# Moving two modulation terms from TensorE to GpSimd in the prologue of a two-layer decoder trunk

## What is computed

```python
cond = jax.nn.silu(c)                          # 1024 values
for l in range(DEPTH):                         # 2 layers
    mod = cond @ w_mod[l] + b_mod[l]           # 1024 x 3072 product with one row
    shift, scale, gate = thirds of mod
    h = rmsnorm(x, norm_g[l]) * (1.0 + scale) + shift
    P = h @ w_in[l]                            # one wide projection, cut into heads
    ...                                        # three mixers, gated and merged
    x = x + gate * (merged @ w_out[l])
return rmsnorm(x, final_g)
```

## Time and profile before

| | |
|---|---|
| runs | 1308.01, 1309.58, 1309.88 us; median 1309.58 |
| the profiled execution's own time | 1307.09 us |
| its span in the trace | 1305.3 us |
| PE busy | 1273.2 us, 98% of the span |
| DVE, ACT, POOL busy | 692.4, 630.3, 719.2 us |
| mean granted PE clock | 0.997 of full |
| first column 0 on PE to the end of the five items | 17.5 to 64.0 us |

### The profile page before, as it was taken

How to read it: one execution, slowest core, us unless ns; L and a number is a source line. 1 busy time by engine, 2 the same in 40 slices (tenths; PEclk the granted TensorE clock), 3 DMA queues, 4 the chain that set the end, 5 groups by cost and what they waited for, 6 DMA issues and landing times.

```text
span 1305.3 us, 16860 instructions
## 1 busy us (share of the span) xinstructions
PE 1273.2 (98%) x5772; PEld 1006.7 (77%) x5772; DVE 692.4 (53%) x1129; ACT 630.3 (48%) x958; POOL 719.2 (55%) x1470
## 2 busy tenths in 40 slices
PE   7999999999999999999999999999999999999996
PEld 4878887787678777788868888778876777778885
DVE  7677767634757234444365777553356533333332
ACT  5366656444553344444245666554455424344441
POOL 3365556774335554576645645576623474546662
PEclk9999999999999999999999999999999999999999
DMA  9432223342223433342222111223311232332331
GB/s 367 148 87 81 65 67 119 113 142 95 73 73 122 133 101 110 101 129 97 97 74 97 66 65 65 90 92 105 112 56 55 83 113 81 93 93 81 97 97 65
DMA packets 40902, 130.51 MB, mean 100 GB/s; under 512 B 5392, under 2 KB 5520, under 8 KB 39536
## 3 DMA queue, kind: packets, MB, share of 16 engines
q1 hardware_dynamic: 30448, 110.22, 25.8%
q10 hardware_dynamic: 10368, 19.21, 5.0%
HBM read 126.33 MB, written 2.10 MB: 98 GB/s over the span
## 4 chain that ended last, share of the span: by engine, by line
PE 89%; DVE 5%; ACT 2%; DMA 1%; POOL 1%; issue 1%; SPq 0%; DVEq 0%; ACTq 0%
PE ps_st L831 22%; PE ps_st L833 22%; PE ps_st L832 22%; PE ps_o L897 5%; PE ps_s L935 3%; PE ps_s L978 3%; PE ps_s L1001 2%; PE ps_misc L892 1%; PE ps_w L987 1%; DMA pro_w<-w_mod_first 1%; POOL w_lo L697 1%; ACT w_hi L1066 1%; PE ps_s L937 1%; PE ps_w L1013 0%; DVE sq_sum L1426 0%
## 5 line engine op out<-in xcount | busy, mean ns | idle before, releaser
L697 POOL TENSOR_TENSOR w_lo<-raw,w_hi 128x128 fp32r<-128x128 f32 x1448 | 708.4, 526 | 563.7 <-ACT w_hi L1066 563.6
L831 PE MATMUL ps_st<-h_hi,w_hi 128*128 128x512 f32 x920 | 372.7, 405 | 3.2 <-POOL w_lo L697 2.7
L833 PE MATMUL ps_st<-h_hi,w_lo 128*128 128x512 f32 x920 | 359.1, 390 | 0.0
L832 PE MATMUL ps_st<-h_lo,w_hi 128*128 128x512 f32 x920 | 358.6, 390 | 0.0
L1066 ACT ACTIVATE w_hi<-raw 128x1024 fp32r<-128x1024 f32 x182 | 190.5, 1047 | 70.9 <-PE ps_st L833 41.2
L831 PEld LDWEIGHTS ps_st<-h_hi,w_hi 128*128 128x128 f32 x920 | 172.9, 188 | 44.9 <-POOL w_lo L697 5.5
L832 PEld LDWEIGHTS ps_st<-h_lo,w_hi 128*128 128x128 f32 x920 | 173.0, 188 | 38.4 <-issue 4.8
L833 PEld LDWEIGHTS ps_st<-h_hi,w_lo 128*128 128x128 f32 x920 | 172.7, 188 | 36.9
L1388 DVE TENSOR_SCALAR gate_x<-ps_st 128x512 f32<-128x512 f32 x79 | 54.4, 689 | 198.2 <-PE ps_st L833 197.9
L1088 ACT ACTIVATE gate_t<-gate_x 128x512 f32<-128x512 f32 x80 | 50.5, 631 | 220.8 <-DVE gate_x L1388 219.9
L1090 ACT ACTIVATE gate_t<-gate_t,cs 128x512 f32<-128x512 f32 x80 | 57.9, 724 | 2.7
(11 more groups left out here) (317 smaller groups left out, 2028.5 us busy)
## 6 DMA issues: line engine op xcount, KB each, us to landing
raw<-w_stream SPq DMA_DIRECT2D x178, 512.0 KB, 3.5
mod_w<-w_mod ACTq DMA_DIRECT2D x64, 256.0 KB, 2.7
pro_w<-w_mod_first SPq DMA_DIRECT2D x8, 1024.0 KB, 16.0
x<-x_t SPq DMA_DIRECT2D x4, 512.0 KB, 7.4
ret_decay<-decay ACTq DMA_DIRECT2D x2, 1024.0 KB, 4.8
out_t<-o_t SPq DMA_DIRECT2D x8, 256.0 KB, 2.9
raw<-w_stream SPq DMA_DIRECT2D x4, 384.0 KB, 3.0
raw_extra<-w_stream SPq DMA_DIRECT2D x2, 512.0 KB, 19.9
```

Of the source, the lines that this page charges most:

```text
L697: ins = nc.gpsimd.tensor_tensor(lo[:, r], whole[:, r], hi[:, r].bitcast(F32), ALU.subtract)
L831: nc.tensor.matmul(dst[0:m, :], wh, hi, start=(k == 0), stop=False)
L832: nc.tensor.matmul(dst[0:m, :], wh, lo, start=False, stop=False)
L833: last = nc.tensor.matmul(dst[0:m, :], wl, hi, start=False, stop=(k == nk - 1))
```

## The change

Terms 6 and 7 of every block go from PE to POOL. A new function `last_terms(j)` on POOL waits for `pro_w[j]`, multiplies both terms by cond into SBUF (`pro_p`, `pro_q`, which lie in `gate_x` and `gate_t`), waits for its own two results, adds them, and signals `pro_part`. It stands twice at the head of POOL's queue, once after each of the first five w_lo, and once more after the fifth. DVE's first term of block j waits for `pro_part`, and adds POOL's partial sum: `tensor_scalar` becomes `scalar_tensor_tensor` with a second operand from SBUF. PE's columns keep only the products with ones.

```diff
+        pro_p, pro_q = gate_x[:, :, 0:2 * P], gate_t[:, :, 0:2 * P]
...
         @block.gpsimd
         def _(pool):
+            def last_terms(j):
+                pool.wait_ge(pro_in[j % MOD_RING], 16 * (j // MOD_RING + 1))
+                if j == 0:
+                    pool.wait_ge(cond_ready, 1)
+                if j >= 2:
+                    pool.wait_ge(pro_mod_done, j - 1)
+                for k in range(DVE_TERMS, DT):
+                    src, by = pro_w[:, j % MOD_RING, k, :], cond[:, k:k + 1]
+                    dst = (pro_p if k == DVE_TERMS else pro_q)[:, j % 2, :]
+                    nc.gpsimd.tensor_scalar(dst, src, by, None, ALU.mult).then_inc(pro_part_link, 1)
+                pool.wait_ge(pro_part_link, (DT - DVE_TERMS) * (j + 1))
+                nc.gpsimd.tensor_tensor(pro_p[:, j % 2, :], pro_p[:, j % 2, :], pro_q[:, j % 2, :], ALU.add).then_inc(pro_part, 1)
+
+            last_terms(0)
+            last_terms(1)
             for layer in range(DEPTH):
...
                     ins.then_inc(w_lo_ready, 1)
+                    if layer == 0 and i < len(BATCH):
+                        last_terms(i + 2)
+                        if i == len(BATCH) - 1:
+                            last_terms(DT - 1)
...
                 def mod_columns(j):
-                    pe.wait_ge(pro_in[j % MOD_RING], 16 * (j // MOD_RING + 1))
-                    if j == 0:
-                        pe.wait_ge(cond_ready, 1)
                     columns_of = [bank["w1"][:, what * DT + j:what * DT + j + 1] for what in range(2)]
                     pe.wait_ge(pro_mod_done, j + 1)
                     for what, dst in enumerate(columns_of):
-                        for k in range(DVE_TERMS, DT):
-                            nc.tensor.matmul(dst, pro_w[:, j % MOD_RING, k, what * P:(what + 1) * P], cond[:, k:k + 1],
-                                             start=(k == DVE_TERMS), stop=False)
                         last = nc.tensor.matmul(dst, pro_acc[:, j % 2, what * P:(what + 1) * P], ones[:, 0:1],
-                                                start=False, stop=True)
+                                                start=True, stop=True)
                     last.then_inc(pro_mod_sum, 1)
...
                         if k == 0:
                             dve.wait_ge(pro_in[j % MOD_RING], 16 * (j // MOD_RING + 1))
-                            link(V.tensor_scalar(acc, src, by, None, ALU.mult))
+                            dve.wait_ge(pro_part, j + 1)
+                            link(V.scalar_tensor_tensor(acc, src, by, pro_p[:, j % 2, :], ALU.mult, ALU.add))
```

More of the change, by code:

```diff
@@ L612, in build @@
         names = ("early_in", "const_in", "pos_in", "par_in", "cond_e", "cond_ready", "pro_link", "pro_mod_done",
-                 "pro_mod_sum", "angles", "tables", "tables_in", "tables_mla", "pro_sq", "fin_sum", "fin_link",
+                 "pro_mod_sum", "angles", "tables", "tables_in", "tables_mla", "pro_sq", "pro_part", "pro_part_link", "fin_sum", "fin_link",
                  "fin_rstd", "fin_wide", "fin_x", "fin_out", "fin_pool", "stored")
         (early_in, const_in, pos_in, par_in, cond_e, cond_ready, pro_link, pro_mod_done, pro_mod_sum, angles, tables,
-         tables_in, tables_mla, pro_sq, fin_sum, fin_link, fin_rstd, fin_wide, fin_x, fin_out, fin_pool, stored) = (sem(n) for n in names)
+         tables_in, tables_mla, pro_sq, pro_part, pro_part_link, fin_sum, fin_link, fin_rstd, fin_wide, fin_x, fin_out, fin_pool, stored) = (sem(n) for n in names)
         pro_in = [sem(f"pro_in{i}") for i in range(MOD_RING)]
```

## The result

| | before | changed |
|---|---|---|
| median of the runs | 1309.69 us (1308.01 to 1309.88) | 1318.9 us (1316.76 to 1321.11) |
| ratio, 95% interval | | 1.0067 (1.005 to 1.0084) |
| the profiled execution's own time, span | 1307.09, 1305.3 | 1318.2, 1316.4 |
| column 7 over (first step behind it starts) | 54.22 us | 63.74 us |
| mean granted PE clock | 0.997 | 0.990 |

The account below looks back on a forecast made before the run. POOL's queue was to set the prologue's pace: 17.4 + 6 x 1.98 + 5 x 4.03 = 49.4 us, then block 6 on DVE and PE's steps to column 7 at 59.6 against 54.22. That is +5.4 us, 1315.0, range 1311.0 to 1319.5.

Parts of the forecast that it names:

- What bounds it, and the mechanism: Prologue: from block 2 on POOL sets the pace, period 6.01 us against DVE's 4.66; column 7 ends 5.4 us later.
- The case with 50%: The forecast itself: L from 1.52 to 2.3 us, without a fall of PE's clock that costs.
- L: Time of POOL's three new instructions per block, two products, a wait and a sum: 1.98 us; shift is 6 L - 6.5 us.
- The price of the product: POOL's 128x256 product with a scalar: 0.43 us, between bounds of 0.155 and 0.70, before the prologue's factor.
- The factor 1.18 for the prologue: POOL is slower in the prologue than at the end, 4.03 / 3.42; the three instructions go from 1.56 to 1.84 us.
- The extra operand on DVE: DVE's first term reads two tensors from SBUF and contends with POOL: up to 0.26 us for block 6, 0.1 counted.
- The columns on PE: Each PE column falls from 1.25 to 0.44 us; columns 3 to 7 save at most 4.05 us.
- Covered work: Later pro_w 6 and 7 transfers cost nothing; POOL's first w_lo ends at 23.4, before PE took it at 23.95, thin cover.
- POOL keeping up: Rival: POOL's instructions overlap or L is below 1.08, so the columns' saving decides: -2.2 us, 1307.4; 4%.
- cheap products: Rival on POOL's products: L from 1.08 to 1.52, 1310 to 1312.2 us; 14%.
- Dear products: Rival: product as dear as a sum or dearer, or contention delaying POOL; L above 2.3, +7.3 us and more; 17%.
- The clock: Rival: PE's waits before columns lower its clock, and behind column 6 that adds 1.7 us, 1316.7; 15%.

Follow-up runs that it names:

- e2: Changed kernel with POOL's new work done but neither waited for nor used by DVE, and PE's columns as before: 1313.37 us, 1.0021 against the kernel before.
- e3: Changed kernel with one 128x512 tensor_tensor on POOL, cond broadcast, in place of the two tensor_scalar products: 1314.67 us, 1.0034 against the kernel before.
- e5: Changed kernel with only term 7 on POOL, no sum, and term 6 kept on PE: ratio 0.9983 against the kernel before.
- e1: Changed kernel with terms 6 and 7 left out altogether, so no POOL part and no DVE wait for it: 1304.38 us, 0.996 against the kernel before.
- e12: The changed kernel measured again unaltered, in more rounds: 1317.24 us, 1.0057 against the kernel before.

## Why the prediction came out as it did

**What bounds it, and the mechanism: right.** The end of the stretch is set by six parts and five w_lo in POOL's queue, then block 6 on DVE, then seven steps and column 7 on PE. The profile after shows this chain step for step, e2 shows that without DVE's wait 5.2 of the 9.5 us go and only 1.9 of the rest is POOL's late w_lo, and e3 and e5 show that DVE's block 6 follows the part's length about sixfold. The case with 50%, L between 1.52 and 2.3, did not come; the one that came had 17%.

**The price of the product: wrong, and the cause of the 4.1 us by which column 7 was missed (63.74 against 59.6).** "The fixed part and half the slope, 0.43, because it reads one tensor where the sum reads two" measured 0.90. Even the upper bound, "0.70, as much as a sum", was broken: there was no row of a `tensor_scalar` on POOL, and a bound taken from another operation is none. The two products were forecast at 0.43 each, or 1.02 with the factor for the prologue, and took 1.80. That L stayed under its upper bound all the same, 2.60 against 2.62, is luck: the products are 0.15 us above their bound of 1.65, and the sum and the wait 0.17 below theirs.

**The factor 1.18 for the prologue: right for w_lo, wrong for the parts.** A w_lo took 4.02 us from start to start, 4.03 in the forecast. The sum was to take 0.70 x 1.18 = 0.83 and took 0.68 to 0.70, and the wait for POOL's own products 0.11 instead of 0.14. DVE stood still while the sum ran (25.2 to 26.94 us in block 2), and the sum took what the line through the earlier trace rows gives, 0.70; in e3, where DVE worked during the sum, it took 1.05. L came out as 0.90 + 0.90 + 0.11 + 0.69 = 2.60 us against 1.98, six times 0.62 is 3.7 of the 4.1 us. Another 0.17 is the transfer of `pro_w` 1, waited for until 17.57 instead of 17.4.

**The extra operand on DVE: right in kind.** The first term took 0.60 instead of 0.49 us (16.61 us, before POOL's w_lo, had 0.49): 0.11, and 0.1 was counted. What was overlooked is `t` in block 6, 1.04 instead of 0.75 while POOL made part 7: 0.3 us.

**The columns on PE: right.** A column took 0.46 and 0.36 us, 0.44 was forecast, and e1 has the whole of PE's saving at -3.7 in its profile, where the bound by DVE and PE together gave -3.0.

**Covered work: right.** No transfer was waited for behind pro_w 1, and the first w_lo, ready at 24.2 and not at 23.4, held nobody up. Its cover was not as thin as the prediction has it: 23.95 in the earlier trace rows is the step's matmul with w_hi, and the one with w_lo started at 25.16 before and at 26.19 after the change.

**The rivals.** POOL keeping up and cheap products are out. "Dear products" is what happened, at the far end (L 2.60, forecast to cost over 7.3 us). The clock came true in part: before column 6 PE was idle for 1.83 us in one profile of the changed kernel, without a fall, and for 2.77 us in e12, with a fall that cost 2.9 us. The Trainium skill (TensorE: Matmul & The Clock Gate, Part 1) has the clock follow how busy the PE was recently; by that rule, more waits are more falls, and the trace agrees: two windows of 7 us at 0.53 and 0.51 and one of 4 us at 0.57 in the changed kernel, against one of 4 us at 0.57 before. Which idle stretch is followed by a fall differs between two profiles of one kernel, as at column 4 in e12 and the first.

**What stays open.** The profiles after the change end 11.1 us later than before, 9.5 of it in the prologue and 1.6 from the fall at 88 us. The medians differ by 9.2 and 7.9. They differ by less than the profiles because the profile before is one of the fastest executions of its kernel, without a fall behind the prologue: its mean granted clock is 0.997, where the later median execution (1309.35) has 0.995. How many falls an average execution of each kernel has, and where, isn't known: each profile shows one execution.

## What to carry to other kernels

Before work is moved to an engine with idle time, add up that engine's queue between the first and the last wait for it, not its share of the span: POOL was 45% idle overall and 20 us in one piece, and had 0.6 to 1.5 us to spare in each period that mattered. Price each new instruction by a row of the same operation on the same engine; where there is none, time it alone first, for neither a cheaper-looking operation nor a dearer one bounds it. And when the offload is good but too slow where it was put, look for another idle engine for its dear half: the same products cost 0.41 us on ScalarE.

## What the runs showed of the hardware

- On GpSimd, `tensor_scalar` of 128x256 fp32 takes 0.90 us with its scalar in SBUF and 0.81 with a constant, while a `tensor_tensor` of the same shape takes 0.68 and one of 128x512 with a broadcast operand 1.04. The Trainium skill (GPSIMD Engine Reference, Engine selection) says that an operation with one input runs roughly at line rate; by that the product would be the cheaper one, which the runs here don't bear out, and the measurement decides. Only this one size was measured, so how much of the 0.90 is a fixed part stays open.
- A stretch at the lower clock costs what the windows show where PE is the bound: 1.7 us for 4 us at 0.57 (at 88 us in the changed kernel), 2.9 us for 8 us at 0.61 (e12). Behind the same idle 2.30 us before column 4 the clock was 0.51 in one execution of the changed kernel and 1.00 in another (e12).
- VectorE and GpSimd slow each other down when both work from SBUF: VectorE's first term of a block takes 0.49 us beside an idle GpSimd and 0.60 beside a w_lo, its `t` 0.75 and 1.04; GpSimd's sum takes 0.69 beside an idle VectorE and 1.05 in e3.
